# Delta rule of a two-layer encoder kernel: levels 1 to 4 of the inverse in 32x32 blocks instead of 64x64, level 5 as a join of two blocks

## The reference, cut to what matters

```python
m = jnp.where(strict, jnp.einsum('bhncd,bhnsd->bhncs', k_beta, k) * decay, 0.0)
eye = jnp.eye(CHUNK, dtype=f32)
t_inv = lax.linalg.triangular_solve(eye + m, jnp.broadcast_to(eye, m.shape), left_side=True,
                                    lower=True, unit_diagonal=True)
u = t_inv @ v_beta
w = t_inv @ (k_beta * jnp.exp(g)[..., None])
```

## Time and profile before

| | us |
|---|---|
| three runs, median (lowest to highest) | 1481.85 (1481.82 to 1484.78) |
| the profiled execution | 1482.01 |
| its span, first to last instruction | 1480.2 |
| PE busy | 1443.7 (98%) |
| DVE busy | 572.0 (39%) |
| ACT busy | 579.2 (39%) |
| POOL busy | 555.1 (38%) |

### The profile page before, as it was taken

The page is one execution under the profiler, slowest core; times in us unless marked ns, Lnnn a source line. Parts: engine busy times, 40 slices in busy tenths (PEclk is TensorE's granted clock), DMA queues, the critical chain, the costliest instruction groups (busy, mean ns, idle before and its releaser), DMA issues.

```text
span 1480.2 us, 22594 instructions
## 1 busy us (share of the span) xinstructions
PE 1443.7 (98%) x8440; PEld 1166.0 (79%) x8440; DVE 572.0 (39%) x1125; ACT 579.2 (39%) x989; POOL 555.1 (38%) x270
## 2 busy tenths in 40 slices
PE   6989999999999999999999999999999999999998
PEld 6867777777777788888888887777788888888887
DVE  3546666666654322221122224674322221022210
ACT  5534544444444443222223234785433322222321
POOL 4533322232321444435443443222254444533432
PEclk9999999999999999999999999999999999999999
DMA  6322110111110233323332233111233223323232
GB/s 242 128 75 75 44 56 31 58 58 58 43 53 22 73 98 114 99 74 109 103 104 95 60 106 120 58 51 44 61 104 113 85 96 92 126 77 108 68 98 77
DMA packets 39223, 124.16 MB, mean 84 GB/s; under 512 B 4192, under 2 KB 5472, under 8 KB 39136
## 3 DMA queue, kind: packets, MB, share of 16 engines
q1 hardware_dynamic: 38976, 122.68, 25.8%
q10 hardware_dynamic: 160, 0.26, 0.1%
HBM read 120.57 MB, written 2.10 MB: 83 GB/s over the span
## 4 chain that ended last, share of the span: by engine, by line
PE 92%; DVE 4%; ACT 2%; issue 1%; DMA 0%; DVEq 0%; SPq 0%; ACTq 0%
PE bank L609 77%; PE bank L806 2%; PE bank L786 2%; ACT ws L1231 1%; PE bank L956 1%; PE bank L928 1%; DVE ws L1699 1%; DVE act_lo L1696 1%; PE bank L1163 1%; PE bank L621 1%; PE bank L1187 1%; PE bank L845 1%; PE bank L1174 1%; PE bank L819 0%; PE bank L758 0%
## 5 line engine op out<-in xcount | busy, mean ns | idle before, releaser
L551 POOL TENSOR_TENSOR w_lo<-w_raw,w_hi 128x1024 fp32r<-128x1024 f32 (+1 forms) x250 | 534.1, 2153 | 796.3 <-ACT w_hi L1231 796.3
L609 PE MATMUL bank<-act_hi,w_hi 128*128 128x512 f32 (+1 forms) x1776 | 709.3, 399 | 6.7 <-DVE act_lo L1696 2.6
L609 PE MATMUL bank<-act_hi,w_lo 128*128 128x512 f32 (+1 forms) x1776 | 681.1, 384 | 0.0
L609 PE MATMUL bank<-act_lo,w_hi 128*128 128x512 f32 (+1 forms) x1776 | 680.0, 383 | 0.0
L609 PEld LDWEIGHTS bank<-act_hi,w_hi 128*128 128x128 f32 x1776 | 335.5, 189 | 76.0 <-issue 7.3
L609 PEld LDWEIGHTS bank<-act_hi,w_lo 128*128 128x128 f32 x1776 | 335.1, 189 | 65.5
L609 PEld LDWEIGHTS bank<-act_lo,w_hi 128*128 128x128 f32 x1776 | 336.0, 189 | 58.3 <-issue 2.9
L1231 ACT ACTIVATE w_hi<-w_raw 128x1024 fp32r<-128x1024 f32 (+1 forms) x250 | 230.6, 953 | 94.5 <-PE bank L609 91.8
L1690 DVE TENSOR_TENSOR ws<-bank,ws 128x512 f32<-128x512 f32 x110 | 75.8, 690 | 333.6 <-PE bank L609 323.3
L1231 ACT ACTIVATE ws<-ws 128x512 f32<-128x512 f32 (+2 forms) x128 | 83.0, 650 | 156.6 <-DVE ws L1690 110.1
L2032 DVE TENSOR_TENSOR xT<-xT,bank 128x512 f32<-128x512 f32 (+1 forms) x48 | 33.0, 688 | 258.6 <-PE bank L609 258.6
(11 more groups left out here) (171 smaller groups left out, 1011.5 us busy)
## 6 DMA issues: line engine op xcount, KB each, us to landing
w_raw<-w_stream SPq DMA_DIRECT2D x154, 512.0 KB, 3.7
w_raw<-w_out SPq DMA_DIRECT2D x32, 384.0 KB, 3.1
w_raw<-w_down SPq DMA_DIRECT2D x32, 384.0 KB, 3.1
w_raw<-w_down SPq DMA_DIRECT2D x32, 320.0 KB, 3.2
ws<-x_in SPq DMA_DIRECT2D x1, 2048.0 KB, 8.8
ws<-mem_in SPq DMA_DIRECT2D x2, 512.0 KB, 4.3
out<-ws SPq DMA_DIRECT2D x1, 1024.0 KB, 4.2
out<-ws SPq DMA_DIRECT2D x1, 768.0 KB, 3.6
```

Source lines behind the costliest of these rows:

```text
L551: nc.gpsimd.tensor_tensor(w_lo[:, s, 0:width * P], w_raw[:, s, 0:width * P], w_hi[:, s, 0:width * P].bitcast(F32), ALU.subtract).then_inc( ...
L609: mm = nc.tensor.matmul(acc, wt[:, c % RING, wsl], at[:, act0(k0 + k), off:off + n], start=(start and k == 0 and m == 0), stop=(stop and k ...
```

## The change

Levels 1 to 4 work on 32x32 blocks: four diagonal blocks q = 0 to 3 of each tile, with rows 32q to 32q+31, packed in 32 columns, so that an operand of all four tiles is 128 columns wide and no longer 256. The two groups g are gone: one wait, 16 matmuls, one signal. Level 5 only joins two neighbouring 32-blocks: 8 products P (rows of blocks 0 and 2) and 12 products Z (4 for the upper half's inverse, 8 for the two transposed off-diagonal blocks). DVE has one multiplication, one subtraction and one transpose in each of the levels 1 to 4, all 128x128; in level 5 it has two copies from PSUM, six copies inside SBUF that unpack the diagonal blocks, and three negations, all of 32 rows. Level 6 keeps its 8 matmuls, with one copy and one negation of twice the width on DVE. Level 0 takes four masked multiplications of 32 rows in place of two of 64. The constants shrink by two squares, and `TT` is cleared once. The diff, cut:

```diff
+        def quarter(q):
+            return slice(QB * q, QB * (q + 1))
...
                 for k in range(1, LEVELS):
+                    quarters, join, last = k < LEVELS - 2, k == LEVELS - 2, k == LEVELS - 1
...
+                    for t in range(NT):
+                        if quarters:
+                            for q in range(4):
+                                mm = nc.tensor.matmul(bank[quarter(q), D[3], QB * t:QB * (t + 1)],
+                                                      key_block(t, q, q), inverse(t, q), start=True, stop=True)
+                        elif join:
+                            for r in range(2):
+                                mm = nc.tensor.matmul(bank[quarter(2 * r + 1), D[3], QB * t:QB * (t + 1)],
+                                                      key_block(t, 2 * r, 2 * r + 1), inverse(t, 2 * r),
+                                                      start=True, stop=True)
...
+                    mm.then_inc(S.p_mm, 1)
+                    fill(10 + 2 * k, 11 + 2 * k)
+                    pe.wait_ge(S.p_done, P_PER_HEAD * h + (k if quarters else LEVELS - 1 if join else LEVELS))
+                    pe.wait_ge(S.y_done, Y_PER_HEAD * h + (Y_PER_HEAD if last else k))
...
+                    for t in range(NT):
+                        if quarters:
+                            for q in range(4):
+                                mm = nc.tensor.matmul(bank[quarter(q), D[4], QB * t:QB * (t + 1)], turned(t, q),
+                                                      masked(t, q), start=True, stop=True)
+                        elif join:
+                            nc.tensor.matmul(bank[quarter(1), D[5], QB * t:QB * (t + 1)], turned(t, 1), masked(t, 1),
+                                             start=True, stop=True)
                             for r in range(2):
+                                q = 2 * r + 1
+                                mm = nc.tensor.matmul(bank[quarter(2 * r), D[4], QB * t:QB * (t + 1)], masked(t, q),
+                                                      turned(t, q), start=True, stop=True)
...
+                    n = (LEVELS - 1) * h + k
+                    dve.wait_ge(S.p_mm, n)
                     if k < LEVELS - 2:
+                        mul(per_tile(w(PM)[:, 0:P]), per_tile(psum(D[3], P)), small(SMALL_LEVEL0 + k)
+                            ).then_inc(S.p_done, 1)
+                        dve.wait_ge(S.tz_mm, n)
+                        sub(w(TT)[:, 0:P], w(TT)[:, 0:P], psum(D[4], P)).then_inc(S.tz_done, 1)
+                        dve.wait_ge(S.tz_done, TZ_PER_HEAD * h + k)
+                        V.transpose(w(TT)[:, P:2 * P], w(TT)[:, 0:P]).then_inc(S.y_done, 1)
+                    elif k == LEVELS - 2:
+                        for q in (1, 3):
+                            cp(ws[quarter(q), PM, 0:P], bank[quarter(q), D[3], 0:P]).then_inc(S.p_done, 1)
+                        dve.wait_ge(S.y_done, Y_PER_HEAD * h + k)
+                        for q in range(2):
+                            cp(per_tile(ws[quarter(q), TT, 2 * P:])[:, :, QB * q:QB * (q + 1)],
+                               per_tile(ws[quarter(q), TT, 0:P])).then_inc(S.y_done, 1)
+                        for q in range(4):
+                            cp(turned_diag(q, q), per_tile(ws[quarter(q), TT, P:2 * P])).then_inc(S.y_done, 1)
+                        dve.wait_ge(S.tz_mm, n)
+                        V.tensor_scalar(per_tile(ws[quarter(1), TT, 2 * P:])[:, :, 0:QB],
+                                        per_tile(bank[quarter(1), D[5], 0:P]), -1.0, None, ALU.mult
+                                        ).then_inc(S.tz_done, 1)
+                        for q in (0, 2):
+                            V.tensor_scalar(turned_diag(q, q + 1), per_tile(bank[quarter(q), D[4], 0:P]), -1.0, None,
+                                            ALU.mult).then_inc(S.tz_done, 1)
```

More of the change, by code:

```diff
@@ L89 @@
 HB = P // 2
+QB = P // 4
 (IDENT, ONES, ONES64, TRIU, NEG_LOWER, SMALL) = range(6)
 SMALL_IDENT, SMALL_LEVEL0 = 0, 1
-N_SQ = SMALL + (1 + LEVELS) // 2
+N_SQ = SMALL + 2
 def squares():
@@ L102, in squares @@
     out[:, NEG_LOWER] = np.where(r <= c, 0.0, -1e30)
-    r, c = r % HB, np.arange(HB)[None, :]
+    r, c = r % QB, np.arange(QB)[None, :]
     small = [r == c, (c == r + 1) & (r % 2 == 0)]
-    small += [(r // 2 ** k % 2 == 1) & (c // 2 ** k == r // 2 ** k - 1) for k in range(1, LEVELS - 1)]
-    out[:, SMALL:].reshape(P, -1)[:, 0:HB * len(small)] = np.concatenate(small, axis=1)
+    small += [(r // 2 ** k % 2 == 1) & (c // 2 ** k == r // 2 ** k - 1) for k in range(1, LEVELS - 2)]
+    out[:, SMALL:].reshape(P, -1)[:, 0:QB * len(small)] = np.concatenate(small, axis=1)
     return out
@@ L789, in delta @@
[L789 to L810, removed]
-                                mm = nc.tensor.matmul(bank[half_rows(r), D[4 + g], z_at], packed(PM, t, r),
-                                                      packed(TT, t, r, 1), start=True, stop=True)
-                        mm.then_inc(S.tz_mm, 1)
@@ L1867, in delta @@
                 dve.wait_ge(S.mt_done, h + 1)
[L1868 to L1876 removed]
+                for q in range(4):
+                    mul(per_tile(bank[quarter(q), D[3], 0:P]), psum4(D[1])[quarter(q), :, QB * q:QB * (q + 1)],
+                        small(SMALL_LEVEL0)[quarter(q)]).then_inc(S.z_pre, 1)
+                dve.wait_ge(S.z_pre, 4 * h + 4)
+                sub(per_tile(w(TT)[:, P:2 * P]), small(SMALL_IDENT), per_tile(psum(D[3], P))).then_inc(S.z_done, 1)
                 dve.wait_ge(S.z_done, h + 1)
[L1878 removed]
+                V.transpose(w(TT)[:, 0:P], w(TT)[:, P:2 * P]).then_inc(S.y_done, 1)
                 if due(h):
@@ L1885, in delta @@
                 for k in range(1, LEVELS):
-                    n = 12 * h + 2 * (k - 1)
-                    for g in range(2):
-                        dve.wait_ge(S.p_mm, n + g + 1)
-                        own = slice(P * g, P * (g + 1))
-                        if k < LEVELS - 1:
-                            mul(w(PM)[:, own].rearrange(pair_c, c=HB), psum(D[3 - g], P).rearrange(pair_c, c=HB),
-                                small(SMALL_LEVEL0 + k, NT // 2)).then_inc(S.p_done, 1)
-                        else:
-                            cp(ws[HB:, PM, own], bank[HB:, D[3 - g], 0:P]).then_inc(S.p_done, 1)
```

121 lines of the change are left out of this document (52 added, 69 removed).

## The result

| | before | after |
|---|---|---|
| median of the runs, us | 1482.15 | 1469.59 |
| lowest to highest of four | 1481.82 to 1484.78 | 1469.18 to 1470.16 |
| the profiled execution, us | 1482.01 | 1469.18 |
| its span, us | 1480.2 | 1467.4 |

The ratio is 0.9911, with a 95% interval of 0.9897 to 0.9926: 12.6 us faster. The prediction was 1467.8 us, with 1459 to 1479 as its range.

What follows compares the result with a forecast made beforehand. PE, busy for 98% of the span, was taken to bound the kernel. Heads 0 to 6 at 1.72 us each (12.0) and head 7 at 2.2 take 14.2 off 1482.0: 1467.8 us, range 1459 to 1479.

Steps and rivals of the forecast that it cites:

- The step: PE, levels 1 to 4: a step at 32 columns takes 32 ns, a group 0.39 us, 0.22 off each.
- Rival 1: PE's small matmuls: a step has a floor at 58 ns, levels 1 to 4 gain 0; 1482 to 1483 us; chance 0.08.
- rival 2: PE's groups: each record costs 27 to 29 ns whatever the block, a group 1.07 us; 1512 us; chance 0.14.
- One bank for four row blocks: PE's groups: two blocks share a bank, four unshown; if they took turns, the time of rival 2, 1512 us.
- DVE behind level 5: DVE's copies, negations and tap delay level 6: P 0.49 us late, gain 0.12 us a head, not 0.91, heads 0 to 6.
- Rival 3: DVE's small operations cost 0.1 us more each, levels 5 and 6 lose 1.0 us a head; 1476 us; chance 0.07.
- The accumulator: Level 3's first fill matmul waits for the accumulator level 2's tap frees: 0.16 us lost in heads 0 to 6.
- Head 7: Last head, without taps: levels 1 to 4 gain 1.76 us, levels 5 and 6 0.46, together 2.2.
- The bounds: Whole kernel: steps of 27 or 45 ns, with the copies' bounds on top, give 1461 to 1477 us.
- The rest: Level 0, clearing of `TT`, ACT and POOL: no effect on the time.

## Why the prediction was right, point by point

- **The step.** 32 ns was read off a line through 58 and 109 ns. Measured it is 0.19 us in six steps of level 5's Z (L821, 182.05 to 182.24 in the rows above), and by the records' starts 31 or 32 ns a step in the groups of four blocks as well. The group was predicted at 0.39 us and is 0.39, in each of levels 1 to 4. Rival 1 (a floor at 58) is out.
- **Records of their own price** (rival 2, 27 to 29 ns each) are out: a step of four records is 31.5 ns, and by the trace their starts lie some 7 ns apart. By the rule of the Trainium skill ("TensorE: Matmul & The Clock Gate", Part 1, "Wait — 56ns, not 53.3ns?": no start within about 25 ns of the last) a group would take 0.95 us, by the prediction's estimate; the measured one is 0.39, and the measurement decides. On one and the same block no two starts came closer than 31 ns here.
- **One bank for four row blocks.** The Trainium skill, "TensorEngine Tiling (Array Packing)", "Gotcha 1: PSUM Pressure", says that different row tiles cannot access one bank at the same time. Here four write it without taking turns: the group's time is that of eight steps, and it is the order of the blocks, with the same bank, that doubles it.
- **DVE behind level 5.** Predicted: copies of 0.23 us 0.26 apart, P of level 6 0.49 late, Z 4.91 us behind level 5's P. Measured: 0.22 and 0.25 (six in 1.46 us), 0.51 late (0.45 of it idle), 185.65 - 180.74 = 4.91. Tap, copies and negations stand in the timeline as summed. Rival 3 is out.
- **The accumulator.** Predicted 0.16, measured 0.22. A group, on the other hand, saved 0.23 us and not 0.22 (1.28 from P to Z for 1.51), eight times a head. The two errors nearly cancel: 1.75 us a head for 1.72.
- **Head 7.** Predicted 2.2, measured 2.33.
- **The bounds.** With steps of 27 ns and the cheaper copies the prediction's own terms come to about 1462.4 us; its 1461 leaves out the accumulator's 0.16. The range doesn't hang on it.
- **The rest** was counted at nothing, and between the levels nothing moved (23.26 us in both). Predicted for the heads 14.2 us, measured 14.6. Between the two profiled executions, from which the sum was made, the time fell from 1482.01 to 1469.18, by 12.8 us: 14.6 in the heads less the 1.7 at the half clock behind L1151, which the profile of after has and that of before has not. The step of the prediction that missed this is the line that counts everything outside the levels at nothing. The median lies another 0.4 us above the profiled execution, within what the runs of one kernel differ by (1.0 us from lowest to highest). The sum rested on one profile, in which that stretch happened to run at the full level; I had looked for the clock only inside the heads, not at the long idle times of PE behind them. That 1467.8 came within 1.8 us of the median owes something to chance here: which of the two levels an execution gets decides 1.7 us.

## What to carry to other kernels

Small block products of plain f32 on the diagonal are paid by the step of one block, 31.5 ns at 32 columns and 58 at 64, with four or two blocks side by side, so long as consecutive instructions go to different blocks; halving the block saved 0.23 us of each group. When a group gets shorter, count at once what the other engine must do until the next one: here 1.1 of 2.85 us a head came back as waits for DVE, and only moving both the tap and the copies brought most of it home (0.71), giving the copies to an idle engine and moving a tap all of it (15.62 us for the levels against 16.72). A single idle stretch of 2.3 us on an otherwise full PE can be followed by another 1.7 us lost at the half clock, in some executions only; look at the granted clock behind each before a difference of 1 or 2 us is explained by an edit.

## What the runs showed of the hardware that I had not expected

- Consecutive matmuls on different 32x32 blocks start some 7 ns apart, and on one block 31 to 32 ns apart. Ordered block by block, the last two or three of a block still run beside the next block's first ones, so that a group in that order costs 0.83 us and not 1.1.
- Small operations on DVE that start at another partition than the one before did not overlap with it: six copies of 0.22 us stand 0.25 apart, while on the same rows the next one starts before the last has ended (two of 0.29 us in 0.52; of 64 rows, two of 0.29 in 0.50). No run changes the start partition alone.
- After 2.3 us without work PE was granted 1.2 GHz for some 3.4 us in six of ten profiles, and 2.4 throughout in four, with the same code ahead of it; that is 1.7 us. After 3.0 us it was 1.2 GHz in twelve of twelve.
- The same six copies take 1.46 us on DVE and 1.98 on ACT.
